# A hybrid trunk with an expert-choice MoE on one core: turning the gathered rows of experts 1 to 15 on VectorE in 32x32 blocks, and the last scatter of a layer in halves

## The reference, cut to what matters

```python
def _expert_choice_ffn(x, router, w_gate, w_up, w_down):
    cap = EC_CAPACITY * T // N_EXPERTS
    xf = x.reshape(T, D)
    aff = jax.nn.softmax((xf @ router).astype(jnp.float32), axis=-1)
    gate, idx = lax.top_k(aff.T, cap)
    xs = xf[idx]
    hid = jax.nn.silu(jnp.einsum('ecd,edf->ecf', xs, w_gate)) * jnp.einsum('ecd,edf->ecf', xs, w_up)
    ye = jnp.einsum('ecf,efd->ecd', hid, w_down) * gate[..., None].astype(x.dtype)
    out = jnp.zeros((T, D), x.dtype).at[idx.reshape(-1)].add(ye.reshape(-1, D))
    return out.reshape(B, S, D)
```

## Time and profile before

| | |
|---|---|
| median of three runs | 2354.94 us |
| the profiled execution: its time, its span | 2355.69 us, 2354.1 us |
| TensorE busy | 2303.9 us, 98% |
| VectorE, ScalarE, GpSimd busy | 995.4, 622.3, 538.7 us |
| HBM read, written | 307.75 MB, 42.28 MB |

### The profile page before, as it was taken

The page is one execution under the profiler, slowest core; times in us unless marked ns, Lnnn a source line. Parts: engine busy times, 40 slices in busy tenths (PEclk is TensorE's granted clock), DMA queues, the critical chain, the costliest instruction groups (busy, mean ns, idle before and its releaser), DMA issues.

```text
span 2354.1 us, 33210 instructions
## 1 busy us (share of the span) xinstructions
PE 2303.9 (98%) x13054; PEld 1644.7 (70%) x13054; DVE 995.4 (42%) x1855; ACT 622.3 (26%) x1445; POOL 538.7 (23%) x550
## 2 busy tenths in 40 slices
PE   8999999999999999999999999999999999999998
PEld 6556587874556888877775665878655568887786
DVE  3654476586554111111136535756864631111111
ACT  3221333553342111111132312335533411111111
POOL 1003453243211111111110034632432111111111
PEclk9999999999999999999999999999999999999999
DMA  4011131221228988778430112312112389878883
GB/s 152 21 37 55 54 131 63 81 81 63 74 96 302 321 280 275 264 266 286 122 124 21 36 54 74 105 54 90 72 73 81 117 290 317 280 255 279 279 284 73
DMA packets 149364, 352.18 MB, mean 150 GB/s; under 512 B 9909, under 2 KB 38073, under 8 KB 149210
## 3 DMA queue, kind: packets, MB, share of 16 engines
q1 hardware_dynamic: 134234, 308.11, 36.6%
q0 software_dynamic: 14976, 41.95, 7.2%
HBM read 307.75 MB, written 42.28 MB: 149 GB/s over the span
## 4 chain that ended last, share of the span: by engine, by line
PE 93%; DVE 2%; DMA 1%; ACT 1%; issue 1%; POOL 0%; SPq 0%; DVEq 0%; ACTq 0%; POOLq 0%
PE ps L1813 88%; PE ps L2349 1%; PE ps L2098 1%; PE ps L2159 1%; PE ps L1832 1%; DVE TMP L1237 1%; DMA HT<-h_sample,idxs 0%; PE ps L1865 0%; DMA y_sample<-SCR,idxs 0%; PE ps L2110 0%; DVE TMP L1246 0%; PE ps L2339 0%; ACT SCR L1042 0%; DVE SCR L1237 0%; POOL SCR L759 0%
## 5 line engine op out<-in xcount | busy, mean ns | idle before, releaser
L1813 PE MATMUL ps<-MID,HT 128*128 128x512 f32 (+3 forms) x2560 | 693.2, 490 | 4.7 <-DMA MID<-w_in 3.8
L1813 PEld LDWEIGHTS ps<-HT,MID 128*128 128x128 f32 x4096 | 557.6, 191 | 16.1 <-issue 15.1
L1813 PE MATMUL ps<-HT,MID 128*128 128x160 f32 (+1 forms) x4096 | 565.6, 299 | 0.6 <-DVE HT L1237 0.4
L1813 PEld LDWEIGHTS ps<-MID,HT 128*128 128x128 f32 (+1 forms) x2560 | 292.6, 157 | 245.8 <-issue 207.2
L1813 PE MATMUL ps<-RING,HT 128*128 128x256 f32 (+2 forms) x1760 | 395.8, 392 | 1.7 <-DVE RING L1241 1.3
L1813 PEld LDWEIGHTS ps<-RING,HT 128*128 128x128 f32 (+1 forms) x1760 | 310.7, 189 | 83.5 <-issue 40.7
L1813 PE MATMUL ps<-HT,RING 128*128 128x512 f32 (+1 forms) x960 | 350.0, 522 | 0.0
L1246 DVE SCALAR_TENSOR_TENSOR HT<-HT,ps 128x160 f32<-128x160 f32 (+1 forms) x128 | 40.9, 319 | 683.1 <-ACT HT L1201 658.5
L1813 PEld LDWEIGHTS ps<-HT,RING 128*128 128x128 f32 x960 | 180.2, 190 | 157.8 <-issue 149.8
L849 POOL DMA_INDIRECT y_prompt<-SCR,idxp x32 | 50.5, 1578 | 618.4 <-ACT SCR L1211 617.8
L1201 ACT ACTIVATE HT<-ps 128x160 f32<-128x160 f32 (+1 forms) x128 | 38.6, 302 | 519.8 <-PE ps L1813 511.5
(11 more groups left out here) (264 smaller groups left out, 2159.3 us busy)
## 6 DMA issues: line engine op xcount, KB each, us to landing
MID<-w_gate SPq DMA_DIRECT2D x32, 2048.0 KB
MID<-w_up SPq DMA_DIRECT2D x32, 2048.0 KB
MID<-w_down SPq DMA_DIRECT2D x32, 2048.0 KB, 15.3
RING<-w_in SPq DMA_DIRECT2D x20, 1024.0 KB, 5.3
SCR<-cs_rows SPq DMA_DIRECT2D x20, 1024.0 KB, 5.1
MID<-w_out SPq DMA_DIRECT2D x8, 1024.0 KB, 6.6
y_sample<-RING SPq DMA_DIRECT2D x16, 512.0 KB, 2.7
h_sample<-HT SPq DMA_DIRECT2D x16, 512.0 KB, 2.6
```

The source lines that it names most:

```text
L1813: return pe.matmul(out, a, b, start=start, stop=stop)
```

## The change

1. TensorE turns only the gathered rows of expert 0 and the first quad, as before (banks 0 and 1). turn_at, quad_at and copied go, and so do the waits on them.
2. For experts 1 to 15 VectorE turns the rows itself, straight from XG to XT. One instruction (turn_rows) takes 32 partitions x 8 blocks of 32x32: those of quadrant a of the tokens and of column block b of each slice k, and writes them to quadrant b of XT, columns 32a on. 16 instructions turn the sample's rows of an expert: eight stand behind the hidden block 1 of the expert before, eight behind block 2; no waits stand between them. Four more turn the prompt's rows of experts 4 to 15 after block 3; experts 1 to 3 still have theirs from XTP by spread_quad.
3. The gain is then applied in place by two operations of four slices each (weigh_tokens), and a new semaphore xt_made tells TensorE and GpSimd that the expert's XT is made.
4. In the last expert of a layer the prompt's down part comes first, then the halves; ScalarE and GpSimd follow in this order; the sample's scatter is made of two, of 128 rows of 2 KB each, with indices 2 i and 2 i + 1 (idxh, two more operations on VectorE behind the indices), and its semaphore counts one scatter more a layer.

The diff, cut to its core (new and changed counters of "halves" in place of "scatter" are left out where they repeat):

```diff
+def prompt_part(e):
+
+    return 3 * e + (3 if e == 0 else 1 if e == E - 1 else 2)
+
+
+def half_part(e, hf):
+
+    if e == 0:
+        return 1 + hf
+    return 3 * e + (2 + hf if e == E - 1 else 1 + 2 * hf)
```

On GpSimd:

```diff
                     def gather(e):
                         if e >= 3:
-                            pool.wait_ge(g_turned, turn_at(e - 3, 1) + 1)
+                            if e == 3:
+                                pool.wait_ge(g_turned, 2)
+                            else:
+                                pool.wait_ge(xt_made, e - 3)
...
                     def gather_quad(q):
                         if q >= 2:
-                            pool.wait_ge(g_turned, quad_at(q - 2, 1) + 1)
+                            if q == 2:
+                                pool.wait_ge(g_turned, 4)
+                            else:
+                                pool.wait_ge(xt_made, QUAD * (q - 1) - 1)
...
+                        if e == E - 1:
+                            pool.wait_ge(scattered_s, seen["halves"] + 16 * e)
+                            for hf in range(2):
+                                pool.wait_ge(down_scaled, 3 * e + 2 + hf)
+                                pool.indirect_dma_start(ys2, bass.IndirectOffsetOnAxis(ap=idxh[:, hf:hf + 1], axis=0),
+                                                        YO[e % 2][:, hf * 512:(hf + 1) * 512], None,
+                                                        compute_op=ALU.add, bounds_check=2 * SEQS[1] - 1).then_inc(scattered_s, 16)
+                            break
```

On ScalarE:

```diff
-                        act.wait_ge(down_part, 3 * e + 1)
+                        if e == E - 1:
+                            scale_prompt()
+                        act.wait_ge(down_part, half_part(e, 0))
                         scale_half(0)
...
-                        else:
+                        elif e < E - 1:
                             scale_prompt()
-                        act.wait_ge(down_part, 3 * e + (3 if e else 2))
+                        act.wait_ge(down_part, half_part(e, 1))
                         scale_half(1)
```

On VectorE:

```diff
                     tt(idxs[:, :], place, ib, ALU.add, idx_ready)
+                    for hf in range(2):
+                        ts(idxh[:, hf:hf + 1], idxs[:, E - 1:E], 2.0, float(hf), ALU.mult, ALU.add)
...
+                    def turn_rows(e, at, rows):
+
+                        for b in range(4):
+                            turned = link(dve.transpose(XT[e % 2][32 * b:32 * b + 32, :, at:at + 32],
+                                                        rows.rearrange("p (k b i) -> p k b i", b=4, i=32)[:, :, b, :]), wait=False)
+                        return turned
+
+                    def turn_tokens(e, a0, a1):
+                        if a0 == 0:
+                            dve.wait_ge(gathered[e % 3], seen["gather"][e % 3] + 16 * (e // 3 + 1))
+                        for a in range(a0, a1):
+                            turned = turn_rows(e, 32 * a, XG[e % 3][32 * a:32 * a + 32, :])
+                        return turned
+
+                    def turn_prompt(e):
+                        q, r = divmod(e, QUAD)
+                        dve.wait_ge(quad_gathered[q % 2], seen["quad"][q % 2] + 16 * (q // 2 + 1))
+                        return turn_rows(e, CAPS, XGP[q % 2][CAPP * r:CAPP * (r + 1), :])
+
+                    def weigh_tokens(e, turned, cols):
+
+                        dve.wait_ge(dve_chain, turned)
+                        for j in range(2):
+                            v = XT[e % 2][:, 4 * j:4 * j + 4, 0:cols]
+                            tt(v, v, wide(pr("gffn")[:, 4 * j:4 * j + 4], cols), ALU.mult, xt_made if j == 1 else dve_chain)
...
-                            if e == 0:
-                                continue
-                            if f == KF - 3 and e + 1 < E:
-                                if (e + 1) % QUAD == 0:
-                                    for j in range(2):
-                                        copy_quad((e + 1) // QUAD, j)
-                                spread_quad(e + 1)
-                            if f == KF - 2 and e + 1 < E:
-                                copy_tokens(e + 1, 0)
+                            if e + 1 < E and 1 <= f <= 2:
+                                turned = turn_tokens(e + 1, 2 * f - 2, 2 * f)
                         if e == 0:
                             for j in range(2):
-                                copy_quad(0, j)
+                                copy_quad(j)
                                 spread_quad(0, 4 * j, 4 * j + 4)
-                            copy_tokens(1, 0)
-                            spread_quad(1)
-                        if e + 1 < E:
-                            copy_tokens(e + 1, 1)
+                        if e + 1 < QUAD:
+                            spread_quad(e + 1)
+                            weigh_tokens(e + 1, turned, CAPS)
+                        elif e + 1 < E:
+                            weigh_tokens(e + 1, turn_prompt(e + 1), TOK)
```

On TensorE:

```diff
                         if e >= 1:
-                            pe.wait_ge(g_copied, copied(turn_at(e, 1) + 1))
-                            pe.wait_ge(quad_spread, e + 2)
+                            pe.wait_ge(xt_made, e)
...
-                            if f == KF - 3 and (e + 1) % QUAD == 0 and e + 1 < E:
-                                for j in range(2):
-                                    turn_quad((e + 1) // QUAD, j)
-                            if f == KF - 2 and 1 <= e < E - 1:
-                                turn_tokens(e + 1, 0)
                         if e == 0:
                             for j in range(2):
-                                turn_quad(0, j)
-                            turn_tokens(1, 0)
-                        elif e + 1 < E:
-                            turn_tokens(e + 1, 1)
+                                turn_quad(j)
...
                             for f in range(KF):
+                                if e == E - 1:
+                                    pe.wait_ge(hid_made, hid_at(KF * e + f))
...
                             prompt_parts()
-                            turn_tokens(1, 1)
                             down_half(1, 0, KF // 2)
...
-                        else:
+                        elif e < E - 1:
                             down_half(0)
                             down_prompt()
+                            down_half(1)
+                        else:
+                            down_prompt()
+                            down_half(0)
                             down_half(1)
```

More of the change, by code:

```diff
@@ L162, in program @@
         idxp = sb("idxp", E, U32)
+        idxh = sb("idxh", 2, U32)
         idxus = sb("idxus", CAPS // 4 + CAPP, U32)
@@ L497, in counts @@
         def counts(layer):
-            return {"x": 16 * layer, "scatter": 16 * E * layer,
+            return {"x": 16 * layer, "scatter": 16 * E * layer, "halves": 16 * (E + 1) * layer,
                     "gather": [16 * layer * len(range(j, E, 3)) for j in range(3)],
@@ L567, in _ @@
                     else:
-                        sp.wait_ge(scattered_s, seen["scatter"])
+                        sp.wait_ge(scattered_s, seen["halves"])
                     for c in range(NP, NC):
@@ L676, in _ @@
                         pool.wait_ge(scattered_p, seen["scatter"])
-                        pool.wait_ge(scattered_s, seen["scatter"])
+                        pool.wait_ge(scattered_s, seen["halves"])
                     for r in RAW:
@@ L862, in _ @@
                         pool.wait_ge(scattered_p, seen["scatter"] + 16 * E)
-                        pool.wait_ge(scattered_s, seen["scatter"] + 16 * E)
+                        pool.wait_ge(scattered_s, seen["halves"] + 16 * (E + 1))
                     leave_layer(pool, layer)
@@ L1203, in _ @@
                             act.wait_ge(scattered_p, seen["scatter"] + 16 * (e - 1))
-                            act.wait_ge(scattered_s, seen["scatter"] + 16 * (e - 1))
+                            act.wait_ge(scattered_s, seen["halves"] + 16 * (e - 1))
                         def scale_half(hf):
@@ L2331, in _, with turn_quad, turn_tokens @@
                     pe.wait_ge(idx_ready, 1)
-                    def turn_quad(q, j):
+                    def turn_quad(j):
                         if j == 0:
-                            pe.wait_ge(quad_gathered[q % 2], seen["quad"][q % 2] + 16 * (q // 2 + 1))
-                        pe.wait_ge(g_copied, copied(quad_at(q, j) - 1))
+                            pe.wait_ge(quad_gathered[0], seen["quad"][0] + 16)
+                        pe.wait_ge(g_copied, 1)
                         pe.wait_ge(h2t_copied, 2 * NC + 1)
                         for k in range(4):
-                            last = pe.transpose(ps[:, j, k * P:(k + 1) * P], XGP[q % 2][:, (4 * j + k) * P:(4 * j + k + 1) * P], ident)
```

(11 more changed lines are left out.)

28 lines of the change are left out of this document (9 added, 19 removed).

## The result

| | before | after |
|---|---|---|
| median, us (4 runs each; before counts one run beside those shown earlier) | 2355.09 (2353.14 to 2355.67) | 2318.01 (2316.75 to 2318.55) |
| span of the profiled execution, us | 2354.1 | 2317.1 |
| TensorE busy, us | 2303.9 | 2273.0 |
| VectorE busy, us | 995.4 | 1239.2 |

The ratio is 0.9842, with a 95% interval of 0.983 to 0.9853 (intervals stand in brackets from here on): 37.1 us faster, with 2317 us forecast.

A forecast was written before the change was run, and what follows sets the result against it. TensorE's queue, busy 98% of the span, was taken as the bound; 24.4 + 5.5 + 3.2 + 3.3 + 2.2 = 38.6 us off the profiled 2355.69 gave 2317 us, range 2311 to 2331.

The forecast's parts named there:

- Turns taken from TensorE: Experts of both layers: TensorE's queue loses eight turns an expert at 0.87 us, 24.4 us, and prompt quads, 5.5 us.
- Turns given to VectorE: Experts 1 to 15's rows: 16 or 20 transposes an expert, estimated 0.45 us each, covered by TensorE's work at no cost.
- The limit of 0.52 us: Longest time per VectorE transpose before the fourth hidden block comes late for the first down half and TensorE waits.
- Expert 0: First expert of each layer: turns of expert 1's rows leave TensorE, less 0.3 us for late VectorE; 3.2 us in all.
- The change of layers: Between the layers: half scatter takes 4.9 us against 8.31 and the prompt's chain moves forward; 3.3 us gained.
- The end: Last scatter of the kernel: a 256 KB half takes 4.9 us instead of 7.17 for the whole; 2.2 us gained.
- The sum: Whole kernel: 24.4 + 5.5 + 3.2 + 3.3 + 2.2 = 38.6 us less, giving 2317 us.
- Partly paid back: Experts: transposes of 0.52 to about 0.61 us delay the fourth hidden block; 2335 us at 0.56 us; chance 0.10.
- VectorE as the bound: Experts 1 to 14: transposes ahead of the fourth hidden block take the whole gain from 0.61 us each; chance 0.08.
- the far case: Experts 1 to 14: transposes far over the limit make VectorE the bound; 2442 us at 0.80 us each.
- The case at 0.80 us: Experts 1 to 14: at 0.80 us a transpose, late hidden blocks cost 125 us, giving 2442 us.
- The weights: Experts: 21.8 us of transfers fit in 26.3 us; late only by contention, then 2347 us; chance 0.04, late gathers included.

The follow-up runs named there:

- The idle turns: Changed kernel plus eight TensorE transposes of a constant, read by nobody, in each of experts 1 to 14: 2343.23 us, ratio 0.9949.
- the extra transposes: Changed kernel with one, two or four unused VectorE transposes added to each group of eight in experts 1 to 14: 2318.77, 2346.21, 2440.60 us.
- the relief: Changed kernel, eight of expert 1's sixteen VectorE transposes moved behind expert 0's quad copies: expert 0 took 23.16 and 23.17 us instead of 23.36 and 23.64.
- the order alone: Changed kernel with the last expert's prompt part still first, but one whole 512 KB sample scatter instead of two halves: 2320.39 us, ratio 0.9853.
- the two other kernels that end with it: Changed kernel with the last expert's old order and whole scatter, 2322.42 us; changed kernel with prompt first and whole scatter, 2320.39 us.
- the run with four extra: Changed kernel with four more unused VectorE transposes in each group of eight in experts 1 to 14: 2440.60 us, ratio 1.0363.
- the two kernels with quarters: Changed kernel, last expert's second half scattered as two quarters: 2316.25 us; the same with VectorE also turning the first quad: 2315.19 us.

## Why the prediction was right

**Turns taken from TensorE** (24.4 + 5.5): right. The idle turns gave 0.88 us for eight where 0.87 was taken, and experts 1 to 15 of the two layers lost 29.84 us where 29.9 were summed. The reading that carried it was the difference of two neighbouring experts and not the duration of a record: by records the same turns would have been 8 x 0.272 = 2.2 us an expert and 61 us in all.

**Turns given to VectorE:** right. A transpose is 436 ns long and starts 467 ns after the one before, where 0.42 and 0.45 us were estimated from rows of other operations; the bounds were 0.29 and 1.3. The limit of 0.52 us was right as a slack too: it means 0.9 us to spare, and the extra transposes found it between 0.93 and 1.87 us. TensorE waits for no hidden block in experts 1 to 14. From 436 ns for a transpose of 256 elements to 826 ns for a tensor_tensor of 640 is 1.02 ns an element, as far as two operations can be set against each other, beside the 1.05 of the tensor_tensor rows: a transpose costs by its elements what those do. The Trainium skill's "Vector Engine (DVE) Microarchitecture Reference" states for it (The reshape front-end and per-opcode configuration) one element a cycle in each lane; the trace fits that if a cycle is about 1.0 ns, which no run here shows. The rule of the Trainium skill's "VectorE: DVE Perf Modes" (Rules for kernel authors), to turn 128x128 blocks on TensorE where PSUM will do, would have left the turns where they were. Here the measurement decides against it: eight of TensorE's turns cost this kernel 0.88 us, and the 16 to 20 instructions of VectorE that replace them cost it nothing as long as they fit into its gaps.

**Expert 0** (3.2): right, 3.43. The 0.3 us a layer that was set aside for a late VectorE is there: 0.40 us of wait in layer 1, and the relief gave 0.20 and 0.47 us back. The +0.40 us at the start belongs to no step of the change: there the granted clock was 0.88 from 730 to 737 us, where it had been 0.95, and 48 matmuls took 6.01 us instead of 5.52. It lies within the spread of that stretch over all executions.

**The change of layers** (3.3): right in size, 3.07, but for partly another cause. It was put down to smaller scatters. The experiment with the order alone shows 2.2 of it to come from the prompt's scatter moving forward, so that SyncE's loads of the prompt's x lie ahead of the last scatter and no longer beside it; the halves are 0.8. The 8.31 us had been read as a scatter "beside other loads", and the prediction did have "the prompt's chain" move 3 us forward; what it did not draw from the two is that these loads then no longer run beside the last scatter. The 4.9 us that it set against the 8.31 were 5.3 here.

**The end** (2.2): this term was mis-sized; it measured 1.1. The step that failed is "By a line through 3.80 and 7.17 a half of 256 KB takes 4.9 us", and then "the gain is 7.17 - 4.9": 3.80 us ran to the landing and 7.17 to the end of the span, which holds 1.1 us of the kernel's own ending behind the landing. That the half landed after the 4.9 us forecast was luck: by a line through the two landings, 3.8 and 6.1 us, it would have been 4.6. The landings by the DMA issues of the last stretch, before:

```profile
y_sample<-SCR,idxs POOLq DMA_INDIRECT x1, 6.1
```

and after:

```profile
y_sample<-SCR,idxh POOLq DMA_INDIRECT x2, 4.9
y_prompt<-SCR,idxp POOLq DMA_INDIRECT x1, 3.8
```

So 6.1 - 4.9 = 1.2 us were to be had, and 1.1 came. That is one pair of executions. The whole scatter landed after 6.4 and 6.5 us in the two other kernels that end with it, and their ends took 8.98 and 9.08 us; in all profiles the end is 8.6 to 9.1 us with the whole scatter and 7.3 to 7.6 with the halves, 1.4 us apart in the mean, still not the 2.2.

**The sum** was 1.6 us too large (38.6 against 37.0 by the spans): 1.1 of the end, 0.4 of the start, 0.2 of the change of layers and 0.1 of the turns, less 0.2 of expert 0. The execution profiled before stood 0.6 us above the median of its kernel's runs, which hid some of that: 2317.0 forecast, 2318.01 measured.

**The rivals.** Partly paid back and VectorE as the bound did not come, since t is 0.467. Their mechanism is real: it sets in between one and two extra transposes in a group. But the price of the far case was too low: with waits of 2.6 us the run with four extra lost some 1.6 us more to the lower clock in 27 of 28 experts. The case at 0.80 us, priced at 2442 us by waits of 4.5 us alone, would by that have been slower still; this was not run. The weights kept up at a share of 0.84; only in the two kernels with quarters did TensorE wait for them, once each and for 0.2 us.

## What to carry to other kernels

Price an instruction in a full queue by the difference of two neighbouring stretches, one with it and one without, not by the duration of its record; here 0.11 us against 0.27. Before work is moved to an engine with room, find the one result of that engine that is next awaited and count what goes in ahead of it: 47% idle was not the limit, the 0.9 us or a little more before one hidden block were. And read a transfer's duration from issue to landing on both sides of a comparison, and ask which other transfers run beside it and whether the change moves them.

## What the runs showed of the hardware that was not expected

- An idle TensorE can cost more than its idle: after waits of 0.72 and 1.06 us the granted clock stayed at 1.00 and the next 42 records took 6.62 us. After 2.59 us it fell to the lower level in 27 of 28 experts, and they took 8.2 to 8.3 us; in one it stayed at 1.00 and they took 6.62. It is most of what lies between the 2394 us expected of that kernel and the 2440.6 measured.
- Alone at the end of a kernel an indirect scatter of 128 rows lands 3.8, 4.7 to 5.0 and 6.1 to 6.5 us after its start with rows of 1, 2 and 4 KB, so a quarter of the bytes still takes some 60% of the time. With rows of 4 KB it took 8.29 us beside two loads of the prompt's rows, and 9.3 in the median in the midst of the experts, beside the loads of the weights.
- Issuing one takes GpSimd 1.55 us and 0.30 to the next for every one of these sizes, so cutting the last half in two gained 1.4 us where 2.5 were expected from its bytes.
